# Attention of a two-block transformer kernel: heads in pairs over row and column halves of the array, in another order of query blocks

## What is computed

```python
ATTN_GROUPS = ((128, 1), (512, 4), (2048, 16))     # window, dilation
for g, (window, dil) in enumerate(ATTN_GROUPS):    # per block of 128 queries
    s = jnp.einsum('bqhd,bqjhd->bqhj', qb, kg) * scale
    s = jnp.where(valid[None, :, None, :], s, -jnp.inf)
    m = jnp.max(s, axis=-1, keepdims=True)
    e = jnp.exp(s - m); den = jnp.sum(e, axis=-1)
    o = jnp.einsum('bqhj,bqjhd->bqhd', e, vg) / den[..., None]
    # outs, lses; then a softmax over the groups' lses weights the outs
```

## Time and profile before

| | |
|---|---|
| median of 3 runs | 979.63 us |
| lowest, highest | 979.19, 980.06 us |
| profiled execution, span from first to last instruction | 980.3 us |
| TensorE matmuls busy | 958.0 us (98%) |
| TensorE weight loads busy | 929.5 us (95%) |
| VectorE busy | 649.5 us (66%) |
| ScalarE busy | 517.7 us (53%) |
| GpSimd busy | 1.1 us |
| HBM traffic | 175 GB/s over the span |

### The profile page before, as it was taken

How to read it: one execution, slowest core, us unless ns; L and a number is a source line. 1 busy time by engine, 2 the same in 40 slices (tenths; PEclk the granted TensorE clock), 3 DMA queues, 4 the chain that set the end, 5 groups by cost and what they waited for, 6 DMA issues and landing times.

```text
span 980.3 us, 19786 instructions
## 1 busy us (share of the span) xinstructions
PE 958.0 (98%) x8781; PEld 929.5 (95%) x8781; DVE 649.5 (66%) x751; ACT 517.7 (53%) x604; POOL 1.1 (0%) x12
## 2 busy tenths in 40 slices
PE   7899999999999999999999999999999999999998
PEld 7899999999999999999899999999889999999998
DVE  2897988774767456566699865437576766466565
ACT  3435454445543569853584541367646654354455
POOL 0000000000000000000000000000000000000000
PEclk9999999999999999999999999999999999999998
DMA  9999557865485443476335432234417266556531
GB/s 340 346 365 320 163 172 257 287 189 173 130 287 187 134 151 104 155 250 190 118 111 155 150 119 58 65 107 130 140 44 237 89 212 216 176 180 203 169 111 44
DMA packets 153440, 172.35 MB, mean 176 GB/s; under 512 B 4000, under 2 KB 137692, under 8 KB 153228
## 3 DMA queue, kind: packets, MB, share of 16 engines
q1 hardware_dynamic: 151696, 167.43, 52.9%
q10 hardware_dynamic: 1660, 3.67, 1.1%
HBM read 170.03 MB, written 1.05 MB: 175 GB/s over the span
## 4 chain that ended last, share of the span: by engine, by line
PE 50%; DVE 5%; ACT 3%; issue 1%; DVEq 0%
PE pj L2570 39%; PE m_all L2295 1%; PE m_all L2297 1%; PE m_all L2284 1%; PE pj L2529 1%; PE pj L2531 1%; ACT w_hi L939 1%; PE pj L2530 1%; DVE w_lo L1429 1%; PE m_all L2022 1%; PE pj L2386 1%; PE m_all L2420 1%; PE m_all L2223 1%; DVE work L1841 0%; PE m_all L2447 0%
## 5 line engine op out<-in xcount | busy, mean ns | idle before, releaser
L1429 DVE TENSOR_TENSOR w_lo<-raw,w_hi 128x2048 fp32r<-128x2048 f32 (+1 forms) x126 | 285.4, 2268 | 127.6 <-ACT w_hi L939 126.9
L2570 PE MATMUL pj<-h_hi,w_hi 128*128 128x256 f32 x1224 | 347.9, 284 | 2.8 <-DVE h_lo L1850 1.1
L2570 PE MATMUL pj<-h_lo,w_hi 128*128 128x256 f32 x1224 | 342.5, 280 | 0.0
L2570 PE MATMUL pj<-h_hi,w_lo 128*128 128x256 f32 x1224 | 342.3, 280 | 0.0
L939 ACT ACTIVATE w_hi<-raw 128x2048 fp32r<-128x2048 f32 (+1 forms) x126 | 237.8, 1890 | 84.9 <-PE pj L2570 68.6
L2570 PEld LDWEIGHTS pj<-h_hi,w_hi 128*128 128x128 f32 x1224 | 229.6, 188 | 8.0 <-issue 5.8
L2570 PEld LDWEIGHTS pj<-h_lo,w_hi 128*128 128x128 f32 x1224 | 229.8, 188 | 0.3
L2570 PEld LDWEIGHTS pj<-h_hi,w_lo 128*128 128x128 f32 x1224 | 229.6, 188 | 0.2
L2570 PE MATMUL pj<-y_hi,w_hi 128*128 128x256 f32 x592 | 166.0, 280 | 1.1 <-issue 0.9
L2570 PE MATMUL pj<-y_lo,w_hi 128*128 128x256 f32 x592 | 165.3, 279 | 0.0
L2570 PE MATMUL pj<-y_hi,w_lo 128*128 128x256 f32 x592 | 165.2, 279 | 0.0
(11 more groups left out here) (401 smaller groups left out, 1201.7 us busy)
## 6 DMA issues: line engine op xcount, KB each, us to landing
raw<-in_odd_in_w_dram SPq DMA_DIRECT2D x28, 1024.0 KB, 5.4
raw<-in_w_in_dram SPq DMA_DIRECT2D x23, 1024.0 KB, 5.3
raw<-in_ada_w_dram SPq DMA_DIRECT2D x22, 1024.0 KB, 6.7
raw<-in_w_ff_in_dram SPq DMA_DIRECT2D x16, 1024.0 KB, 5.4
raw<-in_w_ff_out_dram SPq DMA_DIRECT2D x16, 1024.0 KB, 5.2
raw<-in_even_in_w_dram SPq DMA_DIRECT2D x13, 1024.0 KB, 5.8
raw<-in_even_out_w_dram SPq DMA_DIRECT2D x8, 1024.0 KB, 6.1
raw<-in_odd_out_w_dram SPq DMA_DIRECT2D x8, 1024.0 KB, 5.1
```

Of the source, the lines that this page charges most:

```text
L1429: V.tensor_tensor(lo[:, 0:n], raw_of(u)[:, 0:n], hi[:, 0:n].bitcast(F32), ALU.subtract).then_inc(done, 1)
L2570: m = nc.tensor.matmul(to, a_, b_, start=(s == 0 and q == 0 and (fb == 0 or not together)), stop=(s == len(steps_) - 1 and q == 2), skip_g ...
```

## The change

Attention now works on pairs of heads. Round j of four handles both heads of a pair and one block of queries, in the order (pair 0, block 0), (0, 1), (1, 1), (1, 0). In at_s the matmuls of the two heads alternate between the upper and the lower 64 rows of the array and write different banks; in at_o they alternate between the column halves and write one bank, M[3]. VectorE and ScalarE work head after head, with instructions of the same sizes; a copy of the result is 128 rows high instead of 64. Scores are transposed back into the banks that they came from. The steps stand apart in the list instead of in slots. The first half of the up projection au, its first contraction block for all four jobs, is a step `au_first` of its own before at_o(2), and the weight splits that stood before au0 and after au3 come before it.

```diff
-    at = pipeline(("at_s", "at_t", "at_o"), 2 * AT_H)
     second("wga", "sigmoid", 4000, 3)
-    for st in next(at):
-        step(*st)
+    step("at_s", 0)
     step("rw_gate")
     second("wgb", "sigmoid", 5024, 0)
-    for i in range(1, 4):
-        for st in next(at):
-            step(*st)
-        second("wgb", "sigmoid", 5024, i)
+    step("at_t", 0)
+    second("wgb", "sigmoid", 5024, 1)
+    step("at_o", 0)
+    second("wgb", "sigmoid", 5024, 2)
+    step("at_s", 1)
+    second("wgb", "sigmoid", 5024, 3)
     step("mixed", 0)
     ups = [unit(ins["w_rwkv_up_2"][0], 0, 4, i * CB, 2 * CB) for i in (0, 2)]
+    behind = ((), (("at_t", 1),), (("at_o", 1), ("at_s", 2), ("mixed", 1)), (("at_s", 3),))
     for i in range(4):
-        for st in next(at):
+        for st in behind[i]:
             step(*st)
-        if i == 2:
-            step("mixed", 1)
         job("ru", "up", i, "F", [ups[i // 2]], 4, 0, lambda xc: ("mixed_lo", 1), col=(i % 2) * CB)
-    for n, sts in enumerate(at):
-        for st in sts:
-            step(*st)
-        step("mixed", 2 + n)
+    step("at_t", 2)
     ua = unit(ins["w_attn_up_2"][0], 0, 2, 0, 4 * CB)
+    schedule.append(("au_first", None))
+    for st in (("at_o", 2), ("mixed", 2), ("at_t", 3), ("at_o", 3), ("mixed", 3)):
+        step(*st)
     for i in range(4):
-        job("au", "up", i, "F", [ua], 2, 4, lambda xc: ("mixed_lo", 2 if xc == 4 else 5), col=i * CB)
+        job("au", "up", i, "F", [ua], 2, 4, lambda xc: ("mixed_lo", 2 if xc == 4 else 4), col=i * CB)
         jobs["au", i]["late"] = True
-        if i == 0:
-            schedule.insert(-1, ("split_hi", ("au", 0)))
+    k = schedule.index(("au_first", None))
+    schedule[k:k + 1] = [("split_hi", ("au", 0)), ("split_lo", ("au", 0)), ("step", ("au_first", None))]
...
+        at_pairs = ((0, 0), (0, 1), (1, 1), (1, 0))
+        at_halves = tuple(slice(HD * half, HD * (half + 1)) for half in range(2))
+        at_out = M[3][:, T:T + P]
...
+        def at_bank(j, half, at):
+            k = 2 * half + at // 512 if at_pairs[j][1] else half
+            return M[k], at % 512
...
@@ ScalarE @@
+            def at_s(j):
+                for n in (2 * j, 2 * j + 1):
+                    act.wait_ge(S("at_max"), n + 1)
+                    p = sc(j, n % 2)
+                    nc.scalar.activation(p, p, ACT.Exp, bias=small[:, 20 + n:21 + n], accum_out=small[:, 28 + n:29 + n]).then_inc(S("at_exp"), 1)
+            def at_t(j):
+                for half in range(2):
+                    act.wait_ge(S("at_turned"), 2 * j + half + 1)
+                    if j >= 1:
+                        act.wait_ge(S("at_o"), min(j, 2))
...
@@ VectorE @@
+            def at_s(j):
+                if j >= 2:
+                    dve.wait_ge(S("at_turned"), 2 * (j - 1))
+                dve.wait_ge(S("at_s"), j + 1)
+                for half in range(2):
...
+                    V.tensor_reduce(small[:, 20 + n:21 + n], p, AX.X, ALU.max, negate=True).then_inc(S("at_max"), 1)
+                for half in range(2):
...
+                    V.tensor_scalar(p, p, small[:, 28 + n:29 + n], None, ALU.mult).then_inc(S("at_p"), 1)
...
@@ TensorE @@
+            def at_s(j):
+                if j in (1, 2):
+                    pe.wait_ge(S("at_pt"), pt_done(j - 1))
+                    pe.wait_ge(S("at_oa"), j)
+                if j == 3:
+                    pe.wait_ge(S("at_max"), 6)
+                for g in range(AT_G):
+                    for half, hs in enumerate(at_halves):
+                        bank, at = at_bank(j, half, g * (i + 1) * P)
+                        m = nc.tensor.matmul(bank[:, at:at + (i + 1) * P], q_[hs, 2 * g + hp, i * P:(i + 1) * P], k_[hs, 2 * g + hp, 0:(i + 1) * P], start=True, stop=True)
...
+            def at_t(j):
+                if j >= 2:
+                    pe.wait_ge(S("at_max"), 8)
+                if j == 3:
+                    pe.wait_ge(S("at_pt"), pt_done(2))
...
+            def at_o(j):
+                    pe.wait_ge(S("at_oa"), j)
+                pe.wait_ge(S("at_pt"), pt_done(j))
+                for k in range(total):
+                    for half, hs in enumerate(at_halves):
+                        m = nc.tensor.matmul(at_out[hs], av_tok[:, st, g * AT_W + h * HD:g * AT_W + (h + 1) * HD], pt(j, half)[:, k * P:(k + 1) * P],
...
+            def au_first():
+                split_done(pe, units[ua])
+                for key in au_jobs:
+                    bank_free(key)
+                    au_part(key, 0)
```

More of the change, by code:

```diff
@@ L1195, in gn_mean @@
                 nc.scalar.activation(xx[0:96, 1, :], xx[0:96, 1, :], ACT.Sigmoid).then_inc(S("gate_x"), 1)
[L1197 to L1212, removed]
+            def at_s(j):
[8 more added lines that the diff above has]
+                        act.wait_ge(S("at_o"), min(j, 2))
+                    for a_, b_ in at_spans(j):
+                        bank, at = at_bank(j, half, a_)
+                        i_ = nc.scalar.activation(pt(j, half)[:, a_:b_], bank[:, at:at + b_ - a_], ACT.Copy)
+                        i_.then_inc(S("at_pt"), 1)
+            def at_o(j):
+                hp, i = at_pairs[j]
+                if j == 3:
                     return
-                act.wait_ge(S("at_o"), n + 1)
-                nc.scalar.activation(oa[half, h // 2, i * P:(i + 1) * P], M[1][half, T:T + P], ACT.Copy).then_inc(S("at_oa"), 1)
+                act.wait_ge(S("at_o"), j + 1)
+                nc.scalar.activation(oa[:, hp, i * P:(i + 1) * P], at_out, ACT.Copy).then_inc(S("at_oa"), 1)
             def mixed(part):
@@ L1223, in mixed @@
                     return
[L1224 to L1230, removed]
+                k, t_ = mixed_part(part)
+                act.wait_ge(S("at_o" if part == 3 else "at_oa"), part + 1)
+                nc.scalar.activation(h_hi[:, 4 + k, t_], at_out if part == 3 else oa[:, k, t_], ACT.Copy).then_inc(S("mixed_hi"), 1)
             def root(name, bias=eps_col):
@@ L1831, in rw_gate @@
                 dve.wait_ge(S("rw_out"), 1)
[L1833 to L1845, removed]
+            def at_s(j):
+                if j >= 2:
+                    dve.wait_ge(S("at_turned"), 2 * (j - 1))
+                dve.wait_ge(S("at_s"), j + 1)
+                neg = K(f"at_neg{at_pairs[j][1]}")
+                for half in range(2):
+                    p, n = sc(j, half), 2 * j + half
+                    for a_, b_ in at_spans(j):
+                        bank, at = at_bank(j, half, a_)
+                        link(V.scalar_tensor_tensor(out=p[:, a_:b_], in0=bank[:, at:at + b_ - a_], scalar=float(HD) ** -0.5, in1=neg[:, a_:b_], op0=ALU.mult, op1=ALU.add))
+                    V.tensor_reduce(small[:, 20 + n:21 + n], p, AX.X, ALU.max, negate=True).then_inc(S("at_max"), 1)
+                for half in range(2):
+                    p, n = sc(j, half), 2 * j + half
+                    dve.wait_ge(S("at_exp"), n + 1)
+                    link(V.reciprocal(small[:, 28 + n:29 + n], small[:, 28 + n:29 + n]))
+                    V.tensor_scalar(p, p, small[:, 28 + n:29 + n], None, ALU.mult).then_inc(S("at_p"), 1)
             def mixed(part):
@@ L2404, in rw_gate, with pt_done @@
                         m.then_inc(S("rw_g"), 1)
[L2406 to L2409, removed]
+            def pt_done(j):
+                return sum(2 * len(at_spans(i)) for i in range(j + 1))
+            def at_s(j):
+                hp, i = at_pairs[j]
+                if j == 0:
                     pe.wait_ge(S("roped"), 6)
                     pe.wait_ge(S("gn_c"), 1)
[L2412 to L2416, removed]
+                if j == 1:
+                    pe.wait_ge(S("rw_out"), 1)
+                if j in (1, 2):
[3 more added lines that the diff above has]
+                    pe.wait_ge(S("at_max"), 6)
@@ L2421, in at_s @@
                 m.then_inc(S("at_s"), 1)
[L2423 to L2426, removed]
+            def at_t(j):
+                if j >= 2:
+                    pe.wait_ge(S("at_max"), 8)
+                if j == 3:
+                    pe.wait_ge(S("at_pt"), pt_done(2))
+                for half in range(2):
+                    pe.wait_ge(S("at_p"), 2 * j + half + 1)
+                    for k in range(AT_G * (at_pairs[j][1] + 1)):
+                        bank, at = at_bank(j, half, k * P)
+                        m = turn(bank[:, at:at + P], sc(j, half)[:, k * P:(k + 1) * P])
+                    m.then_inc(S("at_turned"), 1)
@@ L2477, in _ @@
                          key_norms=key_norms, rw_cross=rw_cross, rw_blocks=rw_blocks, rw_join=rw_join, rw_joined=rw_joined, rw_state=rw_state, rw_u=rw_u, rw_t=rw_t,
[L2478 removed]
+                         solve_w=solve_w, solve_u=solve_u, solve_y=solve_y, gn_mean=gn_mean, gn_var=gn_var, rw_gate=rw_gate, at_s=at_s, at_t=at_t, at_o=at_o, au_first=au_first, turn_p=turn_p,
```

71 lines of the change are left out of this document (37 added, 34 removed).

## The result

The changed kernel takes 986.02 us (median of 4 runs, 984.78 to 986.80), the kernel before 979.85 us beside it (979.19 to 980.67). The ratio is 1.0055, 95% interval 1.0042 to 1.0067: slower by half a per cent. The forecast was 986.0.

A forecast was written before the change was run, and what follows sets the result against it. The prediction took TensorE, issuing nearly without a break from 661 to 737 us, as the bound unless VectorE or ScalarE chains come late. It summed 979.6 + 2.4 (waits less saved work) + 4.0 (clock) = 986.0 us, range 980.0 to 990.5.

The forecast's parts named there:

- The work saved: TensorE's score and value steps, paired: 9.5 us of work against 18.6, 9 us saved.
- The first wait: TensorE before ru0, waiting for the chain from s1 to h_lo: 5.9 us where there were 1.1.
- The second wait: TensorE before t2, waiting for the maxima of s3 behind job ru2's split and evacuation on VectorE: 5.0 us.
- The small waits: TensorE's shorter waits: s2 0.4 us, s3 1.5, o3 0.9 for ScalarE's copies, the first second-half job 0.7.
- The clock: Granted clock falls in or right after both long waits, slowing ru0, t2 and part of au_first: +4.0 us.
- The clock holding: Rival: the clock does not fall at the two long waits; 982.0 us; chance 0.20, half of it within 0.2%.
- No overlap: Rival: the array halves don't overlap in the attention steps, so the 9 us aren't saved; 990 us; chance 0.05.
- The wait before t2 not being there: Rival: VectorE's maxima of s3 come ahead of ru2's split and evacuation; 977.1 us, 979 with one fall; chance 0.09.
- The net without the clock: The stage's balance on TensorE: waits up from 3.6 to some 15 us, work down by 9, net +2.4 us.

The follow-up runs named there:

- e9: e4 with TensorE also waiting, in each of the eight steps, for the first half's last matmul before beginning the second: 993.79 us, ratio 1.0129.
- e1: The changed kernel with the split of wo0's weights moved from job ru2 to behind job ru3: 979.91 us, ratio 0.9997.
- e3: The changed kernel with unused filler matmuls in the two long waits, 12 before ru0 and 10 before t2: 981.23 us, ratio 1.0010.
- the first experiments: The first four of the eight follow-up kernels; the kernel before took 980.4 us (27 runs) beside them.
- e2: The changed kernel with at_s(1) one job earlier, directly behind at_o(0) and ahead of wgb2: 981.90 us, ratio 1.0018.
- e4: The changed kernel with the same matmuls one head after the other in at_s and at_o, without alternation: 988.89 us, ratio 1.0085.
- e5: The changed kernel with the first half of the up projection back in its jobs, behind o3: 985.00 us, ratio 1.0044.
- e6: The changed kernel in another order, with s1, t1, o1, s2 and other steps moved between the projections: 975.15 us, ratio 0.9944.
- e8: e6 with the split of wo0 behind t2, which stands behind ru3: 972.43 us, ratio 0.9916.

## Why the prediction was right

**The work saved** was put at 9 us and measured 9.7. That the halves overlap was taken from other lines of the same kernel, and e9 shows the term by itself.

**The first wait** (5.9) measured 5.6. Its chain of 7.1 us was read whole from the trace of before and came back to 0.1 us. **The second wait** (5.0) measured 4.25, with the same order of events and the same cause, which e1 shows by moving the split. The chain from the second exponential's end to t2 took 7.3 us where 7.6 was laid out; the rest is that TensorE came later, behind the first fall of the clock, which the layout of the waits left out. **The small waits** came as laid out: s3 1.3 (1.5), s2 0.5 (0.4), o3 0.8 (0.9), au0's second half 0.7 (0.7). One was not counted by itself: wo0 waits 1.9 us for y_lo where before it waited 0.3. It is VectorE's chain of four merges, which bounds wo0 in both kernels. Its start came 5.7 us later in the stage than before, where 2.4 + 4.0 = 6.4 was laid out.

**The clock** was put at +4.0 us, +2.2 behind the first wait and +1.8 behind the second. The traces show +1.4 and +2.7, and e3 takes back 4.4 to 4.8. So both parts were off, by 0.8 and 0.9 us, and the sum was right because they cancel, which is luck. Three sizes failed. The low level did not last through ru0's 24 matmuls but through 13 and a part of the next. It lasted through 14 of au's first halves and a part of the next, where twelve were assumed. And a transpose was priced at 0.19 us against 0.135, from rows with their changes of form and their last end in them; from start to start it is 0.21 against 0.11, so t2 lost 1.25 us and not 0.7. The Trainium skill, "TensorE: Matmul & The Clock Gate", Part 1, holds that activity releases the throttle: behind both waits the rows at 698 and 726 us, back at 1.00, agree.

**The total** met the measurement to 0.02 us, closer than its terms, and that is luck as well. From its layout the stage should have become 6.4 us longer; the trace shows 5.7 and the ratio 5.4. It was added to 979.63 us, and the kernel before took 979.85 beside the changed one, 980.4 in the 27 runs beside the first experiments.

**The rivals.** The clock holding (982.0) is refuted by the rows and by e3, which is what that case looks like: 981.2. No overlap (990) is refuted, and e9 shows what it would have been: 993.8, the 990 of that case and some 4 us for the clock, which falls there too. The wait before t2 not being there (979 with one fall) did not come, but e1 is nearly that case made: ru2's evacuation still stands ahead, 1.0 us of wait is left, and the time is 979.9. Its condition, the maxima of s3 ahead of the split, was the right one.

**What stayed off.** Both rows on which the prediction judged the clock were read too simply. It said that only at the end does the clock fall. In the same trace it is low from 493.3 to 496.7 us, with TensorE busy throughout and without a wait between 480 and 497 us:

```profile
494.00:496.00 2.00, 2.00 (x11) 2.00 (x11) 1.92 (x3) 1.98 (x5) 0.00 (x0) 0.50 0.95 330
```

Sixteen projection matmuls run at 0.21 us there, some 1.5 us lost. The trace of the changed kernel has the same at 492 us, so it is not in the difference; those of e2, e4, e5 and e6 don't have it, and their stages begin some 1 to 1.5 us earlier than in the changed kernel. Before it stand matmuls that use 32 of the array's 128 rows; what brings the fall in some executions is open. And the 2.9 us of idling at the start, held for a wait without a fall because the row says 1.00, is no such case. The instructions right behind it, in the kernel before, and the same kind in e3's long waits:

```profile
3.14 4.21 PE L2029 MATMUL m_all<-cst 128*128 128x256 f32 x9
...
687.85 5.34 PE L2496 MATMUL pj<-cst 128*128 128x256 f32 x24
```

The first start 0.43 us apart, half the speed of the others with 0.22. The trace's first record of the clock stands at 15.5 us (7.5 in the changed kernel), so the 1.00 before it is no measurement. The fall at the kernel's end, from which the prediction argued that long waits would bring one, did not recur at that point of the work either: in the changed kernel the clock was 1.00 from 976 to 980 us. That the two long waits bring a fall was thus a guess on weak evidence that came true; e3 and e8 show it, since without these waits there was none in the stage.

The net without the clock was put at +2.4 us, while e3 lies 1.0 us over its kernel before, 1.7 in its trace. The 0.7 us more of saved work accounts for the trace's part.

## What to carry to other kernels

Pairing two half-array matmuls halved their time on TensorE, but where such steps feed a chain through VectorE and ScalarE the work saved turns into waits (9.7 us into 11.4 here), until the order is laid out again: the same steps with the chains begun one or two projections earlier, and with a weight split (2.29 us, nobody waits for it) moved from ahead of a maximum that TensorE does wait for, gave 7.9 us. Every wait of 3.0 to 5.6 us in these kernels cost another 1.3 to 2.8 us behind it, since part of the work that followed ran at half speed; where no useful work could be put into it, useless matmuls paid. And before a row of the clock is taken as evidence, compare it with the distance of the starts of equal instructions.

## What the runs showed of the hardware

- Matmuls on different halves of the array overlap without alternating in the list: 120 instructions of them in 13.9 us, against 9.8 alternating and 19.4 kept apart. I had expected no overlap there.
- The two column halves can write to the same PSUM bank at once: at_o's 24 instructions took 1.53 us, as twelve did before.
- In e2 the clock had fallen behind a wait of 3.0 us (ru0 took 4.2 us for 2.8), while waits of 1.4 us left it at 1.00.
- It need not fall within the wait: in e4 t2's twelve transposes ran at 0.11 us each behind a wait of 3.9 us, and the clock fell 1.3 us after t2's start (0.50 from 722 to 724 us, with TensorE busy throughout). Nor does it need a wait: the kernel before at 493 us.
- The low level halves the pace: a projection matmul of 256 columns starts every 0.213 us for 0.118, a transpose every 0.21 for 0.11.
- In e5, with one pair of waits, the time ranged over 5 us along with the mean granted clock (0.995 to 0.987). The Trainium skill, "TensorE: Matmul & The Clock Gate", Part 1, says that the number of slow matmuls differs between runs of one kernel. The traces agree: behind the same wait of 5.6 us, ru0 had 13 slow matmuls in the changed kernel, 14 in e1 and some 20 in e5.
